# The router and the first gather of a mixture-of-experts layer: row scaling on two engines, router weights stationary, one-hots before weights, two gather banks, and the last expert's order

## The reference, cut to what matters

```python
x = x + memory_attention(rms_norm(x, norm_xq[l]), rms_norm(mem, norm_mem[l]), ...)
x = x + hierarchical_moe(rms_norm(x, norm_ffn[l]), w_router_group[l], ...)
return rms_norm(x, norm_final)

def hierarchical_moe(h, w_rg, b_rg, w_re, b_re, w_gate, w_up, w_down):
    t = h.reshape(-1, D)                                   # 256 x 1024
    pg = softmax(t @ w_rg + b_rg)                          # 4 groups
    gate_g, gidx = top_k(pg, 1)
    el = (t @ w_re + b_re).reshape(N, 4, 8)[arange(N), gidx[:, 0]]
    pe = softmax(el)                                       # 8 experts of the chosen group
    pe_top, eloc = top_k(pe, 2)
    wts = gate_g * pe_top / sum(pe_top)
    # each chosen (token, expert) pair:
    y = (silu(x @ w_gate[e]) * (x @ w_up[e])) @ w_down[e]  # 1024 -> 512 -> 1024
    out = sum over the two experts of wts * y
```

## Time and profile before

| | |
|---|---|
| median of three runs | 1873.79 us |
| the profiled execution's own time | 1872.54 us |
| its span | 1870.6 us |
| PE busy | 1707.4 us, 91% |
| DVE busy | 875.3 us, 47% |
| ACT busy | 635.0 us, 34% |
| HBM read | 408.06 MB, 219 GB/s over the span |

### The profile page before, as it was taken

The page is one execution under the profiler, slowest core; times in us unless marked ns, Lnnn a source line. Parts: engine busy times, 40 slices in busy tenths (PEclk is TensorE's granted clock), DMA queues, the critical chain, the costliest instruction groups (busy, mean ns, idle before and its releaser), DMA issues.

```text
span 1870.6 us, 33432 instructions
## 1 busy us (share of the span) xinstructions
PE 1707.4 (91%) x14190; PEld 1423.1 (76%) x14207; DVE 875.3 (47%) x1369; ACT 635.0 (34%) x863; POOL 45.0 (2%) x53
## 2 busy tenths in 40 slices
PE   6998988878878787899999989999899998999998
PEld 5996876545555454699989779998799996579997
DVE  3775442111101110645558665555855557745554
ACT  4543432111011100433444163334343344443332
POOL 2000000000000000000000400000000000000000
PEclk9999989989999999999999999999999999999999
DMA  9534367999999999755544035554355553025550
GB/s 294 178 136 141 141 221 299 418 418 418 418 418 417 417 417 415 263 189 179 184 153 158 1 110 185 187 191 158 116 177 187 188 185 113 23 68 190 191 180 23
DMA packets 190109, 410.05 MB, mean 219 GB/s; under 512 B 6871, under 2 KB 139118, under 8 KB 173660
## 3 DMA queue, kind: packets, MB, share of 16 engines
q1 hardware_dynamic: 188064, 404.55, 59.6%
q0 software_dynamic: 1744, 4.53, 0.8%
q10 hardware_dynamic: 236, 0.06, 0.0%
HBM read 408.06 MB, written 1.05 MB: 219 GB/s over the span
## 4 chain that ended last, share of the span: by engine, by line
PE 70%; DMA 10%; DVE 8%; SPq 6%; ACT 4%; issue 1%; POOL 0%; ACTq 0%; DVEq 0%; POOLq 0%
PE bank L545 18%; PE bank L546 17%; PE bank L547 17%; DMA odd_expert<-in_w_up_dram 9%; SPq L424 6%; PE bank L896 4%; PE bank L866 3%; DVE wlo L1641 2%; PE bank L1037 2%; PE bank L853 2%; PE bank L661 1%; PE bank L885 1%; PE bank L687 1%; DVE prob L1900 1%; ACT whi L1219 1%
## 5 line engine op out<-in xcount | busy, mean ns | idle before, releaser
L2111 DVE TENSOR_TENSOR wlo<-raw,whi 128x2048 fp32r<-128x2048 f32 x120 | 275.1, 2292 | 272.6 <-ACT whi L1514 272.6
L1514 ACT ACTIVATE whi<-raw 128x2048 fp32r<-128x2048 f32 x120 | 229.7, 1914 | 277.5 <-PE bank L547 277.5
L545 PE MATMUL bank<-x1hi,whi 128*128 128x256 f32 x944 | 270.2, 286 | 5.8 <-DVE x1lo L1673 4.7
L546 PE MATMUL bank<-x1hi,wlo 128*128 128x256 f32 x944 | 267.0, 283 | 0.0
L547 PE MATMUL bank<-x1lo,whi 128*128 128x256 f32 x944 | 267.0, 283 | 0.0
L545 PE MATMUL bank<-x0hi,whi 128*128 128x256 f32 x880 | 249.6, 284 | 1.7 <-DVE x0lo L1673 1.7
L546 PE MATMUL bank<-x0hi,wlo 128*128 128x256 f32 x880 | 249.0, 283 | 0.0
L547 PE MATMUL bank<-x0lo,whi 128*128 128x256 f32 x880 | 249.0, 283 | 0.0
L1641 DVE TENSOR_TENSOR wlo<-raw,whi 128x2048 fp32r<-128x2048 f32 x67 | 153.0, 2290 | 92.5 <-ACT whi L1219 92.3
L545 PEld LDWEIGHTS bank<-x1hi,whi 128*128 128x128 f32 x944 | 180.9, 192 | 9.9 <-issue 7.6
L546 PEld LDWEIGHTS bank<-x1hi,wlo 128*128 128x128 f32 x944 | 181.0, 192 | 1.5 <-issue 0.7
(11 more groups left out here) (310 smaller groups left out, 2378.7 us busy)
## 6 DMA issues: line engine op xcount, KB each, us to landing
raw<-in_ffn_w_gate_dram SPq DMA_DIRECT2D x44, 1024.0 KB, 5.4
raw<-in_ffn_w_up_dram SPq DMA_DIRECT2D x44, 1024.0 KB, 5.4
raw<-in_ffn_w_down_dram SPq DMA_DIRECT2D x44, 1024.0 KB, 4.9
raw<-in_w_gate_dram SPq DMA_DIRECT2D x32, 1024.0 KB, 21.4
raw<-in_w_up_dram SPq DMA_DIRECT2D x32, 1024.0 KB, 22.6
raw<-in_w_down_dram SPq DMA_DIRECT2D x32, 1024.0 KB, 22.6
odd_expert<-in_w_gate_dram SPq DMA_DIRECT2D x32, 1024.0 KB, 22.7
odd_expert<-in_w_up_dram SPq DMA_DIRECT2D x32, 1024.0 KB, 22.1
```

Of the source, the lines that this page charges most:

```text
L545: pe.matmul(dst, a_hi, b_hi, start=first, stop=False, skip_group_check=True)
L546: pe.matmul(dst, a_lo, b_hi, start=False, stop=False, skip_group_check=True)
L1514: act.activation(whi[:, c0_ % SPLIT, :], raw[:, c0_ % RAW, :], ACT.Copy).then_inc(hi_ready, 1)
L2111: dve.tensor_tensor(wlo[:, c0_ % SPLIT, :], raw[:, c0_ % RAW, :], whi[:, c0_ % SPLIT, :].bitcast(F32), ALU.subtract).then_inc(lo_ready, 1)
```

## The change: what it does

- The row scaling no longer multiplies by the gain. DVE scales tile 0 and ACT tile 1. The gain goes in as a per-partition column `ffn_gain` where the turned rows are split (`split_turned(1, "ffn")`) and where the gathered rows are copied.
- The router's weights are the stationary side (36 columns), the turned rows the moving side (256 columns), k by k as the low parts come. The 36 x 256 result is copied by DVE and turned back in two transposes.
- The router's weights and the gain column are loaded and split earlier; `norm_final` is loaded earlier.
- The one-hots are made from the indices before the weights; their sum has a tile of its own, `chosen`. Thresholds and weights come after the first selection.
- The gather's halves go to banks 5 and 6. DVE, not ACT, copies them, with the gain.
- ACT's exponential of the difference stands ahead of all copies of the memory tokens.
- `keep_busy` ahead of the turn goes from 14 to 18, ahead of the products from 6 to 2 and in bank 1.
- In the last expert the previous expert's `spread_out` stands between gate and up instead of behind them.

```diff
@@ POOL @@
             pool.wait_ge(h_ready, 1)
-            pool.dma_start(gain_b, ins["norm_ffn"][0].partition_broadcast(P)).then_inc(in_late, 16)
+            pool.dma_start(gain_b, ins["norm_final"].partition_broadcast(P)).then_inc(in_final, 16)
+            pool.dma_start(ffn_gain[:, :], ins["norm_ffn"][0].rearrange("(p k) -> p k", k=KT)).then_inc(in_late, 16)
+            pool.dma_start(wr_raw[:, :, 0:4], ins["w_router_group"][0].rearrange("(p k) n -> p k n", p=P)).then_inc(in_late, 16)
+            pool.dma_start(wr_raw[:, :, 4:36], ins["w_router_expert"][0].rearrange("(p k) n -> p k n", p=P)).then_inc(in_late, 16)
             pool.wait_ge(s_full, 12)
             pool.dma_start(mem2_a, ins["mem_2"][0].rearrange("(t p) d -> p t d", p=P)).then_inc(in_mem2, 16)
-            pool.wait_ge(o_done, 8)
-            pool.dma_start(wr_raw[:, :, 0:4], ins["w_router_group"][0].rearrange("(p k) n -> p k n", p=P)).then_inc(in_late, 16)
-            pool.dma_start(wr_raw[:, :, 4:36], ins["w_router_expert"][0].rearrange("(p k) n -> p k n", p=P)).then_inc(in_late, 16)
-            pool.wait_ge(xn_ready, 10)
-            pool.dma_start(gain_b, ins["norm_final"].partition_broadcast(P)).then_inc(in_final, 16)
@@ PE @@
-            keep_busy(14, ps[4])
+            keep_busy(18, ps[4])
+            pe.wait_ge(r_rows, 1)
             turn(xn, (xn_ready, 10))
-            keep_busy(6, ps[0])
-            x_ready()
+            keep_busy(2, ps[1])
             pe.wait_ge(wr_ready, 1)
+            for k in range(KT):
+                x_part(k, True)
+                mm = split_product(ps[0][0:36, 0:TOK], wr_hi[:, k, :], wr_lo[:, k, :], xhi[1][:, k, :], xlo[1][:, k, :],
+                                   k == 0, k == KT - 1)
+            mm.then_inc(r_cols, 1)
+            pe.wait_ge(r_copied, 1)
             for tt in range(TT):
-                for k in range(KT):
-                    mm = split_product(ps[4][:, tt * 36:tt * 36 + 36], xhi[1][:, k, tt * P:tt * P + P],
-                                       xlo[1][:, k, tt * P:tt * P + P], wr_hi[:, k, :], wr_lo[:, k, :], k == 0, k == KT - 1)
+                mm = pe.transpose(ps[4][:, tt * 36:tt * 36 + 36], logit_t[:, tt * P:tt * P + P], ident[0:36, 0:36])
             mm.then_inc(r_done, 1)
...
-            def gate_up(x_of, parity, arrived, s):
+            def gate_up(x_of, parity, arrived, s, between=None):
                 for which in range(2):
+                    if which == 1 and between is not None:
+                        between()
...
-            gather(0, main, EG * SLOTS, ps[5], sel).then_inc(main["fill"], 1)
-            gather_half(1, 1)
+            for half in range(2):
+                gather(half, main, EG * SLOTS, ps[5 + half], sel).then_inc(main["fill"], 1)
...
-                    gate_up(lambda k: xg[:, k, e * SLOTS:e * SLOTS + SLOTS], e % 2, arrived, main)
+                    final = last and e == EG - 1
+                    gate_up(lambda k: xg[:, k, e * SLOTS:e * SLOTS + SLOTS], e % 2, arrived, main,
+                            (lambda: spread_out(EG - 2, main, 4 * g + EG - 1)) if final else None)
...
-                    else:
+                    elif not final:
                         spread_out(e - 1, main, 4 * g + e)
...
-                    gather_half(0, 4 * g + 4)
+                    pe.wait_ge(main["evac"], 4 * g + 4)
+                    gather(0, main, EG * SLOTS, ps[5], sel).then_inc(main["fill"], 1)
                 spread_out(EG - 1, main, 4 * g + 4)
                 if not last:
-                    gather_half(1, 4 * g + 5)
+                    gather(1, main, EG * SLOTS, ps[6], sel).then_inc(main["fill"], 1)
@@ ACT @@
+            act.wait_ge(in_late, 48)
+            act.activation(wr_hi, wr_raw, ACT.Copy).then_inc(wr_split, 1)
             act.wait_ge(in_mem2, 16)
             row_stats(mem2_a)
             row_stats(h, added(26))
-            act.wait_ge(in_late, 48)
-            act.activation(wr_hi, wr_raw, ACT.Copy).then_inc(wr_split, 1)
-            split_turned(1, None)
+            act.wait_ge(r_scale, 1)
+            act.activation(xn[:, 1, :].rearrange("p (k q) -> p q k", q=P), h[:, 1, :].rearrange("p (q k) -> p q k", k=KT),
+                           ACT.Copy, scale=rstd[:, 1:2]).then_inc(r_rows, 1)
+            split_turned(1, "ffn")
...
-            act.wait_ge(m2_turned, 1)
-            mem2_turned(1, range(6))
             act.wait_ge(r_ediff, 1)
             act.activation(eexp, ediff, ACT.Exp).then_inc(r_eexp, 1)
-            mem2_turned(1, range(6, KT))
+            act.wait_ge(m2_turned, 1)
+            mem2_turned(1, range(KT))
             mem2_turned(0, range(KT))
@@ DVE @@
-            row_scale()
-            dve.wait_ge(in_late, 48)
-            for tt in range(TT):
-                dve.scalar_tensor_tensor(xn[:, tt, :].rearrange("p (k q) -> p q k", q=P),
-                                         h[:, tt, :].rearrange("p (q k) -> p q k", k=KT), rstd[:, tt:tt + 1],
-                                         gain_b.rearrange("p (q k) -> p q k", k=KT), ALU.mult, ALU.mult).then_inc(xn_ready, 1)
...
-            split_turned(1, None)
...
+            dve.reciprocal(rstd, root).then_inc(r_scale, 1)
+            dve.wait_ge(r_scale, 1)
...
+            dve.tensor_scalar(xn[:, 0, :].rearrange("p (k q) -> p q k", q=P), h[:, 0, :].rearrange("p (q k) -> p q k", k=KT),
+                              rstd[:, 0:1], None, ALU.mult).then_inc(xn_ready, 2)
+            split_turned(1, "ffn")
+            dve.wait_ge(r_cols, 1)
+            dve.tensor_copy(logit_t, ps[0][0:36, 0:TOK]).then_inc(r_copied, 1)
             dve.wait_ge(r_done, 1)
...
             dve.tensor_tensor(ediff, emax[:, 1:16:8], emax[:, 0:16:8], ALU.subtract).then_inc(r_ediff, 1)
+            dve.wait_ge(r_ediff, 1)
+            for tt in range(TT):
+                dve.tensor_scalar(hot[:, tt, :], slot_row, eidx[:, 2 * tt:2 * tt + 1], None, ALU.is_equal)
+                ins_ = dve.tensor_scalar(hot2[:, tt, :], slot_row, eidx[:, 2 * tt + 1:2 * tt + 2], None, ALU.is_equal)
+            link(ins_)
+            dve.tensor_tensor(chosen, hot[:, :, :], hot2[:, :, :], ALU.add).then_inc(hot_ready, 1)
...
+            link(dve.tensor_reduce(tmax, ps[5][:, 64:96], AX, ALU.max))
...
+            select(0, main["sel"])
+            link(dve.tensor_scalar(thr, cst[:, C_THR:C_THR + 8], tmax, None, ALU.is_lt))
...
             dve.wait_ge(r_exp, 1)
             link(dve.reciprocal(ggate, gsum))
...
+            def copy_gathered(half, count):
+                dve.wait_ge(main["fill"], count)
+                gains = ffn_gain[:, 4 * half:4 * half + 4].unsqueeze(2).broadcast_to([P, 4, EG * SLOTS])
+                dve.tensor_tensor(xg[:, 4 * half:4 * half + 4, :], ps[5 + half][:, :].rearrange("p (k n) -> p k n", k=4), gains,
+                                  ALU.mult).then_inc(main["evac"], 1)
+            copy_gathered(0, 1)
+            copy_gathered(1, 2)
...
             with dve.Fori(0, EXPERTS // EG - 1) as g:
                 expert_group(g, False)
+                copy_gathered(0, 4 * g + 5)
+                copy_gathered(1, 4 * g + 6)
```

More of the change, by code:

```diff
@@ L305, in build @@
         rope_half, rope_sin = sem("rope_half"), sem("rope_sin")
+        r_scale, r_rows, r_cols, r_copied = [sem(n) for n in ("r_scale", "r_rows", "r_cols", "r_copied")]
         wr_ready, r_done, r_bias, r_exp, r_ediff, r_eexp, hot_ready, pos_done, extra_ready = [sem(n) for n in (
@@ L342, in chunk_slot, with gain_col @@
             return raw[:, c % RAW, :].rearrange("p (k n) -> p k n", k=KT if kind == "cols" else 2)
+        def gain_col(gain, k):
+            return ffn_gain[:, k:k + 1] if gain == "ffn" else cols[:, gain + k:gain + k + 1]
         def expert_slot(parity, slot):
@@ L843, in _ @@
                 for i, (lhs, tt) in enumerate(pairs):
-                    mm = pe.matmul(ps[5][:, at_:at_ + 32], lhs, hot[:, tt, :], start=i == 0, stop=i == len(pairs) - 1,
+                    mm = pe.matmul(ps[5][:, at_:at_ + 32], lhs, chosen[:, tt, :], start=i == 0, stop=i == len(pairs) - 1,
                                    skip_group_check=True)
@@ L899, in spread_out @@
                 mm.then_inc(s["spread"], 1)
-            def gather_half(half, count):
-                pe.wait_ge(main["evac"], count)
-                gather(half, main, EG * SLOTS, ps[5], sel).then_inc(main["fill"], 1)
             def turn_spread(half, count):
@@ L1254, in split_turned @@
                         ins_ = act.activation(xhi[x][:, k, :], fill_bank(fill)[:, kk * TOK:kk * TOK + TOK], ACT.Copy,
-                                              scale=1.0 if gain is None else cols[:, gain + k:gain + k + 1])
+                                              scale=1.0 if gain is None else gain_col(gain, k))
                     ins_.then_inc(xhi_ready, 1)
@@ L1440, in copy_piece @@
                                ps[5][:, 0:2 * PIECE].rearrange("p (t n) -> p t n", t=2), ACT.Copy).then_inc(m2_evac, 1)
```

(19 more changed lines are left out.)

46 lines of the change are left out of this document (21 added, 25 removed).

## The result

The changed kernel takes 1863.88 us (median of 4, 1861.09 to 1866.96) against 1873.51 (4 runs) for the kernel before: ratio 0.9946, 95% interval [0.9931, 0.9962]. So it is 9.6 us less, where 12.9 were forecast. The time lies inside the range, 2.9 above the point.

A forecast was written before the change was run, and what follows sets the result against it. The expert stage was taken as bound by weight transfers, so an earlier stream start and a shorter tail count: 5.5 + 4.9 + 2.5 = 12.9 us, giving 1861; range 1858 to 1867, the forecast itself 1858.5 to 1863.

The forecast's parts named there:

- Part 1: Norm to router logits: row copies on two engines and wide products bring the bias earlier; 5.5 us gained (5.3 to 6.2).
- DVE's surcharge of 0.70: Row copies: DVE's extra time for the strided write over contiguous, added to ACT's 1.15 for 1.85, taken as 1.9 us.
- Part 2: Picks to gather: one-hots before weights 3.7, threshold count off the chain 0.5, gather's second half not waiting 0.7; 4.9 us.
- its largest term: Picks: one-hots made straight from the indices, without waiting for ACT's exponential and the weights; 3.7 us gained.
- Part 3: Tail: previous expert's sums between gate and up, so the last down starts on w_down's landing; 2.5 us gained, perhaps 1.6.
- Behind the experts PE's two mem_2 products go along: Tail: the mem_2 products follow the last expert, bringing the turn to 774.50 - 2.5 = 772.0.
- just covered: Tail: final norm's rows, not moving, ready at 772.33 against the turn at 772.0, second tile's half 1 us later.
- A: Rival: clock at 0.5 over the mem_2 transposes and fillers behind the logits; 4.0 us given back, 1865; chance 0.17.
- C: Rival: clock stays at 1.2 GHz from the turn to the first expert; 1876.6, or 1879 without the tail; chance 0.05.
- D: Rival: expert stream starts early but its end doesn't follow, a slot being freed too late; 1868; chance 0.05.
- B: Rival: the tail gives nothing, as w_down lands at 753 or the norm becomes the bound; 1863.4; chance 0.08.

The follow-up runs named there:

- g3: Changed kernel with both row copies read and written in sequence, the regrouping by every eighth column moved to PE's transposes and gather; 1865.67 us.
- f2: Changed kernel with the gate weights back ahead of the one-hot sum and ACT's exponential behind six mem_2 copies; 1867.74 us.
- e4: Changed kernel without PE's block for overflowing experts, and so without the jump over it; 1859.61 us.
- e3: Kernel before with only the last expert's new order (previous expert's sums between gate and up); 1875.86 us, ratio 1.0013.
- g1: Changed kernel with 5 matmuls of the first mem_2 product moved ahead of PE's jump over the overflow block; 1861.48 us.
- g4: Changed kernel with 5 mem_2 matmuls ahead of the jump, row copies shared 5 to 11 and read in steps, six fillers before the last down; 1858.29 us.
- f1: Changed kernel with half of the first mem_2 product (8 matmuls) moved ahead of PE's jump over the overflow block; 1863.72 us.

## Why the prediction was right, and where the sum was off

- **What bounds it.** This was right. SP's first load came 10.05 us earlier, the last down 12.34, with the same 418 GB/s between.
- **Part 1**, 5.5 forecast, 5.23 measured. The row copy was taken at 1.9 with an upper bound of 2.0; it took 2.23 to 2.52 us. Carrying DVE's surcharge of 0.70 over to ACT was the mis-sized term: ACT pays 1.1 to 1.4 for the same pattern (g3). By the Trainium skill (ScalarE: Activation LUTs, What ACT_TABLE_LOAD costs) the copy would take an estimated 1.13 us; the measurement confirms that for rows in sequence (1.15, g3) and contradicts it for rows with a step. The rest held: from the turn to the last low part 5.45 us (5.46 forecast), the bias 9.54 behind the copies (9.3).
- **Part 2**, 4.9 forecast, 5.00 measured; f2 gives its largest term alone at 2.4 by the chain and 1.7 by the clock, 4.06 where 3.7 stood. What was taken for a wait behind ACT was in part a slow PE, so that the total agrees is in part luck. The ranks came 4.92 behind the bias (5), with 0.47 to spare on PE.
- **Part 3**, 2.5 forecast. Down started on its weights' landing, 1.5 to 2.3 us nearer to the stream's start in the profiles with the new order: right. The step that failed is the next one, "Behind the experts PE's two mem_2 products go along": the first matmul behind the jump came 6.7 us after the first sum, which held them up by 3.18 us (e4: without the jump they do go along). Nothing in the sum, and no rival, had the jump or the fetching of code in it. And in this profile down ran near half clock after its wait, 1.29, which was costed nowhere; the clock was watched only in the router. What it said of the norm held. Counted from the stream's start, as Part 3 counts, the norm's rows were ready at 478.17 us before (772.33 - 294.16), 479.26 after and 478.28 in e4. And "just covered" was close: in e4, where the idle time is gone, the turn starts at 761.08 and the rows are ready at 761.04, so the norm would bound the tail next.
- **Rivals.** A, the half clock over the mem_2 transposes, did not come (1.00 over 254 to 282). Neither did C: the transposes ran at full clock in the changed kernel throughout. Neither did D: the stream's end followed its start, C being 2.29 us shorter and not longer. But f2 shows C's mechanism in small, and e3 does in the old router: a longer wait on PE and the work behind it is at half clock. B's 1863.4 is close to what was measured, by another cause: the tail did give its 2.3, and lost it again.
- **The range.** 1863.88 is above the 1863 up to which the forecast itself was to hold. It is in the range because that was widened for A and D, neither of which came; that two unpriced costs of 4.5 us together fitted there is luck.

So of the 12.9 the three forecast gains gave 12.5. Less 3.2 (the jump) and 1.3 (the clock), plus 0.65 outside these stretches, that is the 8.7 of the spans. e3 adds what a forecast of the parts one by one would have missed: the new order, worth 2.6 to 4 us in the changed kernel, costs the kernel before 2.4 to 3.1 us by itself.

## What to carry to other kernels

A block that is jumped over may not be free: look for "issue" time behind it, also when another edit has only moved the code around it, since one kernel here paid nothing and eleven others did. Leaving the block out took the idle time away (e4, 2.6 us); queueing more matmuls directly ahead of it took away 1.85 us in the profile (g1). Removing a wait on a chain can pay twice, since TensorE's clock stays up over what follows; a wait that a reordering creates elsewhere must be priced by the same rule. An engine's price for a stepped access isn't another engine's: measure it on the engine that is to do the work.

## What the runs showed of the hardware

- The first matmul behind a taken jump on PE started 6.64 to 6.70 us after the first of 8 passes queued ahead of the jump, in nine profiles, with DMA at 355 to 364 GB/s over that stretch. It started 1.48 to 1.51 us behind the end of a 16 KB packet of the instruction queue in all twelve profiles with idle time. In the kernel before, with the same block, the packet came ahead of the 8 passes and nothing was idle.
- With 18 or more passes queued ahead of the jump the idle time was 1.0 to 1.8 us instead of 3.0 (g4, g1, f1). By the packets' starts in f1 (8.2 us behind the first sum) and g1 (4.4, against 4.0 to 4.1 elsewhere) PE's sequencer ran an estimated 17 to 18 passes ahead.
- A step of 32 bytes (reading) or 512 bytes (writing) makes ACT's 128x1024 copy 2.15 to 2.52 us instead of 1.15. DVE's takes 1.15 (reading) and 1.46 to 1.61 (writing) against 0.76.
- PE's moving side takes a step of 32 bytes at almost no cost (16 transposes, 2.03 us against 1.97), its weights don't: 32 gather products take 7.76 us instead of 3.73, both at a granted clock of 1.00.
- After waits of 2.2 to 3.0 us for the last w_down, half clock (0.50, 1.2 GHz) covered 2.6 to 9.4 us of the stretch behind them in seven of ten profiles, and none of it in the other three, whose waits were as long (2.62 to 2.67).
